# Two small buffers of a one-core transformer kernel padded to other lengths

## What is computed

```
for i in (0, 1):
    x = x + 0.5 * swiglu_ffn(rms_norm(x, norm_g[i, 0]), ffn_w_gu[i, 0], ffn_w_down[i, 0])
    h = rms_norm(x, norm_g[i, 1])
    x = x + (gla_mixer(h) if i == 0 else diff_mixer(h))
    x = x + 0.5 * swiglu_ffn(rms_norm(x, norm_g[i, 2]), ffn_w_gu[i, 1], ffn_w_down[i, 1])

def swiglu_ffn(h, w_gu, w_down):            # 1024 -> 2 x 2816 -> 1024
    gate, up = jnp.split(h @ w_gu, 2, axis=-1)
    return (jax.nn.silu(gate) * up) @ w_down
```

## Time and profile before

| | |
|---|---|
| three runs | 2305.47, 2309.34, 2311.35 us; median 2309.34 |
| the profiled execution | 2308.53 us, of which the span from first to last instruction is 2306.7 |
| mean granted TensorE clock | 0.992 of full speed |
| busy share of the span | TensorE 98%, its weight loads 78%, VectorE 55%, ScalarE 39%, GpSimd 7% |
| the chain that ended last | TensorE 89%, VectorE 6%, ScalarE 3%, issue 2% |

### The profile page before, as it was taken

How to read it: one execution, slowest core, us unless ns; L and a number is a source line. 1 busy time by engine, 2 the same in 40 slices (tenths; PEclk the granted TensorE clock), 3 DMA queues, 4 the chain that set the end, 5 groups by cost and what they waited for, 6 DMA issues and landing times.

```text
span 2306.7 us, 24697 instructions
## 1 busy us (share of the span) xinstructions
PE 2252.1 (98%) x9842; PEld 1799.0 (78%) x9842; DVE 1270.6 (55%) x1970; ACT 906.2 (39%) x1402; POOL 154.0 (7%) x127
## 2 busy tenths in 40 slices
PE   7999999899899999999999999999899999999999
PEld 6888887776677888888888887777688888877777
DVE  6443445777754434455433445877566535655763
ACT  4222333545433222233322324777533223237662
POOL 2000002000040000020000012000030000020000
PEclk9999999999999999999999999999999999999999
DMA  5323224021023323233223224222135433232211
GB/s 187 101 82 110 96 69 148 19 92 55 26 80 128 117 91 110 82 101 109 82 83 128 78 80 133 71 71 89 37 112 163 139 117 128 89 126 73 74 55 37
DMA packets 201746, 217.39 MB, mean 94 GB/s; under 512 B 4968, under 2 KB 194536, under 8 KB 201632
## 3 DMA queue, kind: packets, MB, share of 16 engines
q1 hardware_dynamic: 194960, 193.48, 25.9%
q0 software_dynamic: 6528, 22.26, 2.9%
q10 hardware_dynamic: 144, 0.08, 0.0%
HBM read 213.66 MB, written 6.32 MB: 95 GB/s over the span
## 4 chain that ended last, share of the span: by engine, by line
PE 89%; DVE 6%; ACT 3%; issue 2%; DMA 0%; SPq 0%; DVEq 0%; ACTq 0%
PE ps L1574 88%; PE ps L1578 1%; DVE sb_wlo L1043 1%; ACT sb_whi L607 1%; DVE sb_gla_ek L1280 0%; DVE sb_gla_at L1295 0%; DMA sb_raw<-ffn_w_gu 0%; ACT sb_xh L607 0%; DVE sb_xl L1048 0%; DVE sb_gla_eq L1283 0%; DVE sb_gla_xb L1275 0%; DVE sb_gla_d L1262 0%; ACT sb_hyb_th L607 0%; DVE sb_gla_on L1206 0%; ACT sb_gla_z L607 0%
## 5 line engine op out<-in xcount | busy, mean ns | idle before, releaser
L1574 PE MATMUL ps<-sb_xh,sb_whi 128*128 128x512 f32 x2120 | 849.2, 401 | 22.7 <-DVE sb_xl L1048 9.8
L1574 PE MATMUL ps<-sb_xh,sb_wlo 128*128 128x512 f32 x2120 | 831.1, 392 | 0.0
L1574 PE MATMUL ps<-sb_xl,sb_whi 128*128 128x512 f32 x2120 | 830.7, 392 | 0.0
L1043 DVE TENSOR_TENSOR sb_wlo<-sb_raw,sb_whi 128x1024 fp32r<-128x1024 f32 (+2 forms) x401 | 475.2, 1189 | 524.6 <-ACT sb_whi L607 523.4
L607 ACT ACTIVATE sb_whi<-sb_raw 128x1024 fp32r<-128x1024 f32 (+2 forms) x401 | 387.2, 968 | 604.9 <-PE ps L1574 596.4
L1574 PEld LDWEIGHTS ps<-sb_xh,sb_whi 128*128 128x128 f32 x2120 | 402.0, 190 | 117.8 <-issue 17.1
L1574 PEld LDWEIGHTS ps<-sb_xl,sb_whi 128*128 128x128 f32 x2120 | 401.8, 190 | 86.9 <-issue 6.0
L1574 PEld LDWEIGHTS ps<-sb_xh,sb_wlo 128*128 128x128 f32 x2120 | 401.1, 189 | 85.9
L1574 PE MATMUL ps<-sb_ffn_ah,sb_whi 128*128 128x512 f32 x704 | 277.6, 394 | 0.0
L1574 PE MATMUL ps<-sb_ffn_ah,sb_wlo 128*128 128x512 f32 x704 | 276.0, 392 | 0.0
L1574 PE MATMUL ps<-sb_ffn_al,sb_whi 128*128 128x512 f32 x704 | 273.3, 388 | 0.0
(11 more groups left out here) (249 smaller groups left out, 1775.6 us busy)
## 6 DMA issues: line engine op xcount, KB each, us to landing
sb_raw<-ffn_w_gu SPq DMA_DIRECT2D x86, 1024.0 KB, 5.2
sb_raw<-ffn_w_down SPq DMA_DIRECT2D x32, 1024.0 KB, 4.9
sb_raw<-gla_w_in SPq DMA_DIRECT2D x12, 1024.0 KB, 5.3
sb_raw<-diff_w_in SPq DMA_DIRECT2D x12, 1024.0 KB, 5.1
sb_ada_raw<-w_ada POOLq DMA_DIRECT2D x12, 1024.0 KB, 6.4
sb_raw<-w_in SPq DMA_DIRECT2D x10, 1024.0 KB, 5.3
sb_raw<-ffn_w_down SPq DMA_DIRECT2D x16, 512.0 KB, 3.5
sb_raw<-ffn_w_down SPq DMA_DIRECT2D x16, 256.0 KB, 2.7
```

The costliest lines, as they stand in the source:

```text
L1043: e.tensor_tensor(lo, raw[panel % NRAW][:, 0:nk, off:off + 128], hi.bitcast(F32), ALU.subtract).then_inc(sem["w_lo"], 1)
L1574: return e.matmul(out, lhsT, rhs, start=start, stop=stop, skip_group_check=skip)
```

## The change

`par` gets 160 columns instead of 149, in SBUF and in DRAM; the 11 added ones are zero and nothing reads them. `ada` gets 32 columns instead of 24, and nothing uses the added eight. No instruction is changed, except that the load of `par` moves rows of 640 bytes. All later tiles get other starts.

```
 ):
     COLS[_name] = (_n, _k)
     _n += _k
-NCOLS = _n
+NCOLS = -(-_n // 32) * 32
...
         sqs = sb("sqs", [128, S])
         sq = sb("sq", [128, S])
         small = sb("small", [128, 96])
-        ada = sb("ada", [128, 24])
+        ada = sb("ada", [128, 32])
         lam = small[:, 56:64]
         ones, ident, blk = cst[:, 0, :], cst[:, 1, :], cst[:, 2, :]
```

## The result

The changed kernel takes 2316.16 us (median of 9 runs, 2315.09 to 2317.58) against 2309.56 us for the kernel before (9 runs, 2305.47 to 2312.61): 6.6 us or 0.3% slower, ratio 1.003 with an interval of 1.0021 to 1.004. The forecast was 2304 us with a range of 2298 to 2313. The time lies outside the range, and it moved the other way.

The account below looks back on a forecast made before the run. TensorE bounds the kernel, time being matmuls times their step. Stage tiles give back 5.6 us, all other terms nothing: 2303.7 us against the median of 2309.3, given as 2304, range 2298 to 2313.

Parts of the forecast that it names:

- Stage tiles as moving operands: FFN down projections, last projection and diff scores: matmuls at 226.6 instead of 228.9 ns, 4.9 + 0.4 + 0.3 us gained.
- I take the gain of 5.6: Choice of the full 5.6 us for moved stage tiles, between bounds of nothing and a 6.2 us loss; chance 0.53.
- the new start is worse: Rival: the same 2304 stage-tile matmuls get slower at a multiple of 256, up to 6.2 us, 2315.5 us; chance 0.10.
- The last output projection: Last stage, 192 matmuls on stage tiles: 2.2 ns less each, 0.4 us gained.
- The score matmuls of diff: Diff stage, 128 matmuls reading `dif_k` and `dif_kl`: 2.3 ns less each, 0.3 us gained.
- The shared tiles: `cst`, `sq` and others starting 32 bytes beyond a multiple of 64: moving them gains nothing; far bound 8.4 us.
- Slow starts after a change of operand: First 11 matmuls after a down projection take 2.55 instead of 2.49 us; taken as no gain, bound 5 us.
- more than that comes back: Rival: the slow starts after a change of operand go too, 5 us more, 2298.7 us; chance 0.10.
- The bound of 5 us: Most that slow starts could give back: 36 gla score groups and 68 transpose groups at some 0.05 us each.
- GpSimd and par's load: GpSimd's adds of `sq` into `sqs` and `par`'s larger transfer (0.3 us): both hidden, costing nothing.
- the bad case: The rival in which the new start is worse: 2315.5 us, chance 0.10; the range leaves out about half of it.

Follow-up runs that it names:

- the run at 142,208: The kernel before with only `ada` widened to 72 columns, so that stage memory begins at 142,208: 2300.42 us, ratio 0.9965.

## Why the prediction was wrong

What bounds the kernel: right. The kernel's time is the number of matmuls by their step. The difference of 2.3 ns between down and gate and up that I read from the earlier trace rows was real and came from where the moving tiles lie against the weights; the run at 142,208 removed it, and the down projections gave back 4.7 us where I had 4.9.

The step that failed is "Stage tiles as moving operands", and in it the choice "I take the gain of 5.6". It rested on reading the good places as multiples of 128. The reason that I gave, two families of tiles with one remainder and one rate, says that the place matters and nothing of what a third place does. The trace of before had only two places for moving tiles, 128 and 192, and one for weights, 128. From these I could tell that the place matters, and not whether it is the tile's own or its place against the weights. The runs decide for the second. At 142,080 the distance is 128: 233.3 ns, a loss of 8.5 us in the down projections where I had a gain of 4.9.

The rival "the new start is worse" had the mechanism, word for word: "If the equal remainder is what runs free, the change doesn't restore it." It got 0.10. Its price of 6.2 us was too low, since it came from the greatest duration of one product: 5 ns in place of 2.3, so 2.7 more, where the step rose by 4.4 in the stretch of the earlier trace rows. The down projections alone cost 8.5. That the measured 6.6 us lie close to this price is luck: less time at 1.2 GHz, in the gla stage of the profile by 3.4 us, gave part of the loss back. My sum had no term for the granted clock.

The rule of the Trainium skill that I weighed ("SBUF — State Buffer", section Specifications, on lines of 16 bytes) would have left the time at 2309.3. Measured, starts that are all multiples of 16 differ by up to 6.6 ns a matmul, so it doesn't cover this case. It says nothing of two reads that run beside each other. Another part of that page of the Trainium skill, in its section "Who interferes with whom", holds that PE never waits on anyone, and lists two read ports for it, one for the moving operand and one for the loads of weights, as independent. Whether TensorE waits for the reads of other engines no run here tests. But the pace of its matmuls depends on where the two tiles lie against each other, as moving `wlo` alone showed (226.7 to 231.1 ns in gate and up). That the two reads get in each other's way is the likely reason; the runs show the dependence, not the way it comes about.

Point by point. *The last output projection:* it became slower, not faster: its last 84 starts, from 2290.65 to 2309.93 us, are 232.3 ns apart, where it was 228.8. *The score matmuls of diff* can't be told apart from noise: that stage is 0.5 us shorter. Their moving and their weight tiles are both stage tiles and moved together, so by what the runs showed they had nothing to gain or lose; the 0.3 us that I gave them had no ground. *The shared tiles:* nothing, as forecast (2308.87 against 2308.19 us). *Slow starts after a change of operand:* I took nothing. With stage memory at 142,208, TensorE in order of time at the end of the second block of down projections:

```profile
376.98 0.39 PE L1574 MATMUL ps<-sb_ffn_ah,sb_wlo 128*128 128x512 f32 x1
377.21 0.39 PE L1574 MATMUL ps<-sb_xh,sb_whi 128*128 128x512 f32 x1
...
379.93 0.39 PE L1574 MATMUL ps<-sb_xh,sb_whi 128*128 128x512 f32 x1
```

The 13 starts from 377.21 to 379.93 are 226.7 ns apart from the first on: no slow starts there. So these starts do depend on addresses, as the rival "more than that comes back" had it, but only behind the down projections, seven times 0.05 us. Behind scores, transposes and other work hardly anything moved: 138 stretches of 12 matmuls with `xh` and `xl` have a median of 2.59 us from first to last start, 2.61 before, and a mean of 2.69 in both. The bound of 5 us was far off. *GpSimd and par's load:* nothing, as forecast. *The range:* it covered the bad case only by half, with a price that was too low.

What stays open: why 64 is cheaper than all other distances than 0, and which load meets which stream. Also what decides when the granted clock falls. In the profiles of the kernels whose gate and up run at 226.7 ns, the gla stage takes 435.3 us with 17.1 us of it at 1.2 GHz, 435.9 to 436.2 with 20.5 us (six kernels), 438.1 to 438.3 with 23.9 us (four) and 440.2 with 30.7 us. The kernel before and the one with only the shared tiles moved have their stage memory in the same place and yet 23.9 and 30.7 us. So the clock explains the 2.0 us, and I don't put its choice down to the place of the stage tiles.

## What to carry to other kernels

Where TensorE streams one tile while it loads weights from another, give both the same start modulo 256 bytes; here that took 192 bytes of padding and gave 4.7 us in the down projections (7.8 of 2308 us between the medians, the granted clock's part included). Padding to a round number isn't alignment of anything: this change put the stage tiles on a multiple of 256 and moved them away from the weights, which lay 128 beyond one. And when a trace shows that something depends on addresses, list every address that takes part in it before choosing one: a trace with one place for the weights can't tell "at 128" from "level with the weights".

## What the runs showed of the hardware

- The distance from one 512-column matmul to the next was 226.7 ns at the full clock when moving tile and weight slot had the same remainder by 256, 228.9 ns when the moving tile lay 64 bytes above, and 232.3 to 233.3 ns at 32, 96, 128, 192 and 224.
- It depends on the difference and not on the tile's own place: one address of the stage tiles gave 233.3 ns with the weights at 128 and 226.6 ns with the weights at 0.
- The period is 256 (128 isn't free): with stage memory at 142,208 and weights at 49,280 the starts differ by 256 modulo 512, and the step is 226.7.
- The pattern within the three products (394, 388, 392 ns) belongs to the distance 64 and came back with it at other addresses.
- With the low weights alone 128 bytes off, the product that reads and loads only high weights kept 389 ns and the two others had 396 and 397.
- Behind a down projection at distance 64 the next 11 steps of matmuls whose tiles lie level took 2.55 us instead of 2.49; behind one at distance 0 they took 2.49.
- The gla stage, with the same 1828 matmuls, took 438.1 us with 23.9 us at 1.2 GHz and 436.1 us with 20.5.
